# The pair swap of rotary embedding: a TensorE product replaced by four transfers issued from ScalarE

## The reference, cut to what matters

```python
def apply_partial_rope(x, cos, sin):           # layer a: the first 16 of 64 channels of a head
    half = ROPE_DIM // 2                       # 8
    x1, x2 = x[..., :half], x[..., half:ROPE_DIM]
    return concatenate([x1 * c - x2 * s, x2 * c + x1 * s, x[..., ROPE_DIM:]])

def rope(t, cos, sin):                         # layers 0 and 1: all 64 channels
    half = t.shape[-1] // 2                    # 32
    t1, t2 = t[..., :half], t[..., half:]
    return concatenate([t1 * cos - t2 * sin, t2 * cos + t1 * sin])
```

## Time and profile before

| | |
|---|---|
| device time, median of 3 (lowest to highest) | 2407.13 us (2404.87 to 2409.15) |
| the profiled execution's own time | 2409.83 us |
| its span, first to last instruction | 2407.0 us |
| mean granted TensorE clock | 0.978 |
| TensorE products busy | 2235.1 us (93%), 9994 instructions |
| VectorE busy | 1167.8 us (49%), 1815 instructions |
| ScalarE busy | 931.0 us (39%), 1577 instructions |
| GpSimd busy | 1138.5 us (47%), 1364 instructions |
| mean busy share of the 16 DMA engines, queue of SyncE / of ScalarE | 24.4% / 0.6% |

### The profile page before, as it was taken

How to read it: one execution, slowest core, us unless ns; L and a number is a source line. 1 busy time by engine, 2 the same in 40 slices (tenths; PEclk the granted TensorE clock), 3 DMA queues, 4 the chain that set the end, 5 groups by cost and what they waited for, 6 DMA issues and landing times.

```text
span 2407.0 us, 27365 instructions
## 1 busy us (share of the span) xinstructions
PE 2235.1 (93%) x9994; PEld 1697.5 (71%) x9994; DVE 1167.8 (49%) x1815; ACT 931.0 (39%) x1577; POOL 1138.5 (47%) x1364
## 2 busy tenths in 40 slices
PE   6899888998898999999999999889999999999996
PEld 4676556864465766888888788666668888887885
DVE  6786858237635434015319754363340153197542
ACT  3545633235533444233223731334442332237322
POOL 3563226541134422557547475443234575475751
PEclk8999999999999999999999999999999999999998
DMA  3222113220022212332232232212123322232321
GB/s 129 70 88 62 36 53 97 88 79 27 27 62 79 79 53 79 96 106 88 81 103 97 71 108 88 84 53 70 53 73 103 96 92 87 93 105 63 113 88 61
DMA packets 52981, 191.43 MB, mean 80 GB/s; under 512 B 6000, under 2 KB 6256, under 8 KB 52336
## 3 DMA queue, kind: packets, MB, share of 16 engines
q1 hardware_dynamic: 51552, 184.44, 24.4%
q10 hardware_dynamic: 1296, 5.24, 0.6%
HBM read 187.56 MB, written 2.10 MB: 79 GB/s over the span
## 4 chain that ended last, share of the span: by engine, by line
PE 77%; DVE 8%; ACT 6%; POOL 4%; issue 3%; DMA 2%; ACTq 0%; DVEq 0%; SPq 0%
PE proj L516 20%; PE proj L518 19%; PE proj L517 19%; POOL lower L468 4%; PE turned L512 3%; PE stat L512 2%; PE score L512 2%; PE score L516 2%; PE score L517 2%; PE score L518 2%; PE mix L512 2%; DMA raw_ring<-stream 2%; DVE small L1571 1%; PE ptp L727 1%; PE proj L512 1%
## 5 line engine op out<-in xcount | busy, mean ns | idle before, releaser
L468 POOL TENSOR_TENSOR lower<-raw_ring,upper 128x256 fp32r<-128x256 f32 x1360 | 1138.3, 870 | 1225.1 <-ACT upper L1062 1225.0
L516 PE MATMUL proj<-h,upper 128*128 128x512 f32 x1504 | 613.0, 408 | 30.4 <-issue 16.8
L518 PE MATMUL proj<-h,lower 128*128 128x512 f32 x1504 | 589.8, 392 | 0.0
L517 PE MATMUL proj<-h,upper 128*128 128x512 f32 x1504 | 589.0, 392 | 0.0
L1062 ACT ACTIVATE upper<-raw_ring 128x1024 fp32r<-128x1024 f32 x340 | 356.0, 1058 | 564.8 <-PE proj L516 373.3
L516 PEld LDWEIGHTS proj<-h,upper 128*128 128x128 f32 x1504 | 285.0, 189 | 96.6 <-issue 27.9
L518 PEld LDWEIGHTS proj<-h,lower 128*128 128x128 f32 x1504 | 284.1, 189 | 61.3
L517 PEld LDWEIGHTS proj<-h,upper 128*128 128x128 f32 x1504 | 285.2, 190 | 57.2 <-issue 4.3
L516 PE MATMUL proj<-y,upper 128*128 128x512 f32 x632 | 256.8, 406 | 10.8 <-ACT yf L1139 3.7
L518 PE MATMUL proj<-y,lower 128*128 128x512 f32 x632 | 252.0, 399 | 0.0
L517 PE MATMUL proj<-y,upper 128*128 128x512 f32 x632 | 251.6, 398 | 0.0
(11 more groups left out here) (368 smaller groups left out, 3246.7 us busy)
## 6 DMA issues: line engine op xcount, KB each, us to landing
raw_ring<-stream SPq DMA_DIRECT2D x340, 512.0 KB, 3.5
x<-x_in SPq DMA_DIRECT2D x4, 512.0 KB, 6.4
rows<-rows_in ACTq DMA_DIRECT2D x2, 1024.0 KB, 5.2
out<-x SPq DMA_DIRECT2D x8, 256.0 KB, 2.0
memraw<-mem_in SPq DMA_DIRECT2D x1, 1024.0 KB, 10.7
memraw<-mem_in ACTq DMA_DIRECT2D x1, 1024.0 KB, 4.8
rot<-tables_in ACTq DMA_DIRECT2D x2, 512.0 KB, 3.6
ws<-ws_in ACTq DMA_DIRECT2D x2, 256.0 KB, 5.6
```

What stands on the lines that cost most here:

```text
L468: ins = nc.gpsimd.tensor_tensor(lower[:, p % RING, a:b], raw_ring[:, p % RAWS, a:b], upper[:, p % RING, a:b].bitcast(FP32), ALU.subtract)
L516: first_ = nc.tensor.matmul(o, lhsT[0], rhs[0], start=start, stop=False)
L517: nc.tensor.matmul(o, lhsT[0], rhs[1], start=False, stop=False)
L518: return first_, nc.tensor.matmul(o, lhsT[1], rhs[0], start=False, stop=stop)
```

## The change

The permutation is no longer a product. `turn` and the wait for the bank `turned` are gone from TensorE's program. ScalarE gets a function `swap`, which issues four transfers from `nrm` to a second place in SBUF (`home`): `yf1` in layer a, `raw` in the layers 0 and 1, two buffers each. In layer a a transfer moves 8 partitions of 2 KB (16 KB); in the layers 0 and 1 it moves 32 partitions (64 KB). In layer a only 32 of the 128 rows are written, and one VectorE instruction clears both buffers beforehand. VectorE's `rotate` waits for the transfers instead of the product and reads `home` instead of the bank.

```diff
+        def swap(S, C, n, home, half):
+            m = C.next("turn")
+            act.wait_ge(*S.after("nrm", n))
+            if m >= 2:
+                act.wait_ge(*S.after("turned_used", m - 2))
+            src, dst = nrm[:, n % 2, :], home[:, m % 2, :]
+            for at in (0, half, HD, HD + half):
+                to = at + half if at % HD == 0 else at - half
+                act.dma_start(dst[to:to + half, :], src[at:at + half, :]).then_inc(swap_landed[m % 2], 16)
...
-        def heads(S, C, n, cols=SEQ, together=False):
-            for i in range(n + 1):
+        def heads(S, C, n, cols=SEQ, together=False, rotated=0):
+            n0 = C.n["head"]
+            for i in range(n + 2 if rotated else n + 1):
...
+                if 0 <= i - 2 < rotated:
+                    swap(S, C, n0 + i - 2, yf1, 8)
-                if i:
+                if 0 < i <= n:
                     root(S, C, 1.0 / HD, cols)
...
             def take_head():
                 k = C.next("head")
                 take(S, C, nrm[:, k % 2, :], keys_=[("nrm", k)], waits=[("nrm_used", k - 2)] if k >= head0 + 2 else [])
+                swap(S, C, k, raw, 32)
...
-        def rotate(S, C, n, dst, *keys_):
+        def rotate(S, C, n, dst, home, *keys_):
             m = C.next("turn")
             t = nrm[:, n % 2, :]
-            dve.wait_ge(*S.after("turned", m))
-            link(S, nc.vector.tensor_tensor(tmp[:, :], turned[:, :], rot[:, 1, :], ALU.mult), ("turned_used", m))
+            dve.wait_ge(swap_landed[m % 2], 64 * (m // 2 + 1))
+            link(S, nc.vector.tensor_tensor(tmp[:, :], home[:, m % 2, :], rot[:, 1, :], ALU.mult), ("turned_used", m))
...
+        link(S, nc.vector.memset(yf1[:, 0:2, :], 0.0))
...
-        def turn(S, C, swap, n):
-            m = C.next("turn")
-            pe.wait_ge(*S.after("nrm", n))
-            if m:
-                pe.wait_ge(*S.after("turned_used", m - 1))
-            mm(turned[:, :], swap, nrm[:, n % 2, :], True, True).then_inc(*S.mark("turned", ("turned", m)))
```

More of the change, by code:

```diff
@@ L302, in build @@
     stored = nc.alloc_semaphore("stored")
+    swap_landed = [nc.alloc_semaphore(f"swap_landed{r}") for r in range(2)]
     signals = Signals(nc, "run", plans)
@@ L644, in added_squares, with heads @@
             mm(stat[:, :], c("ones"), sq[:, t % 2, :], False, True).then_inc(*S.mark("summed", ("sq_used", t), ("sums", m)))
-        def turn(S, C, swap, n):
-            m = C.next("turn")
-            pe.wait_ge(*S.after("nrm", n))
-            if m:
-                pe.wait_ge(*S.after("turned_used", m - 1))
-            mm(turned[:, :], swap, nrm[:, n % 2, :], True, True).then_inc(*S.mark("turned", ("turned", m)))
-        def heads(S, C, W, jobs, rotate, cols=SEQ, together=None):
-            n0 = C.n["head"]
+        def heads(S, C, W, jobs, cols=SEQ, together=None):
             C.n["head"] += len(jobs)
-            def rotated(i):
-                if 0 <= i < rotate:
-                    turn(S, C, c("swap_a"), n0 + i)
             def summed():
@@ L670, in heads @@
                 jobs[4]()
-                rotated(0)
                 summed()
@@ L674, in heads @@
                 jobs[5]()
-                rotated(1)
-                rotated(2)
                 summed()
@@ L680, in heads @@
                     jobs[i]()
-                rotated(i - 3)
                 if i:
@@ L692, in attention @@
                 pe.wait_ge(*S.after("read", C.n["job"] - j))
-            if C.n["turn"]:
-                pe.wait_ge(*S.after("turned_used", C.n["turn"] - 1))
             def scores(kind, z, t, e, i):
@@ L778, in memory @@
             hkey = lambda k: ("h", f"mem{l}", k)
-            heads(S, C, W, [lambda i=i: full(S, C, W, f"mem{l}.k{i}", mh, hkey, MEM) for i in range(2)], 0, MEM)
+            heads(S, C, W, [lambda i=i: full(S, C, W, f"mem{l}.k{i}", mh, hkey, MEM) for i in range(2)], MEM)
             tokens(S, C, W, names(f"mem{l}.v", 2), mh, hkey, MEM, 2)
@@ L786, in pe_program @@
                 heads(S, C, W, [lambda n=n: full(S, C, W, n, h, hkey)
-                                for n in names("a.q", MT) + names("a.k", MT) + names("a.qm", 2)], 2 * MT,
+                                for n in names("a.q", MT) + names("a.k", MT) + names("a.qm", 2)],
                       together=lambda: group(S, C, W, names("a.q", 4), h, hkey))
@@ L803, in pe_program @@
                 hkey = lambda k: ("h", "b", k)
-                heads(S, C, W, [lambda n=n: full(S, C, W, n, h, hkey) for n in names("b.qm", 2)], 0)
+                heads(S, C, W, [lambda n=n: full(S, C, W, n, h, hkey) for n in names("b.qm", 2)])
                 for n in names("b.q", MT):
@@ L852, in pe_program @@
             full(S, C, W, "kr", h, None)
-            C.next("head")
-            turn(S, C, c("swap_b"), C.n["head"] - 1)
             for t in range(2):
@@ L874, in up @@
                     pass
[L876 to L882, removed]
+            for t in range(LH // 2):
+                up(QR * t, QR, 0)
             for t in range(2):
@@ L1238, in act_program @@
             if s == "a":
-                heads(S, C, 2 * MT + 2, together=True)
+                heads(S, C, 2 * MT + 2, together=True, rotated=2 * MT)
             else:
@@ L1531, in head_units @@
                 if 0 <= i - 2 < rotated:
-                    rotate(S, C, n0 + i - 2, dsts[i - 2], ready[i - 2])
+                    rotate(S, C, n0 + i - 2, dsts[i - 2], yf1, ready[i - 2])
                 if i < len(dsts):
@@ L1762, in dve_program @@
             dve.wait_ge(*S.after("nrm", n))
-            rotate(S, C, n, kr[:, :], ("tails_ready",))
+            rotate(S, C, n, kr[:, :], raw, ("tails_ready",))
             C.n["job"] += 2 * TB + LH
@@ L1767, in dve_program @@
                 n = C.next("head")
-                rotate(S, C, n, qr[:, t, :], ("tails_ready",))
+                rotate(S, C, n, qr[:, t, :], raw, ("tails_ready",))
             C.n["job"] += 2 * LH
```

## The result

The changed kernel takes 2426.24 us (median, 2425.13 to 2428.59). The kernel before, run beside it, takes 2406.68. The ratio is 1.0079 (95% interval 1.0065 to 1.0093): it is slower by 19.6 us, where 2406.0 was forecast and the range ended at 2416. The traced execution's span is 2426.8 us against 2407.0.

What follows compares the result with a forecast made beforehand. TensorE, with 77% of the chain, was taken as the bound where it is late; +6.9 us in layer a less 2 x (1.55 + 2.4) in layers 0 and 1 gave -1.0, forecast 2406.0 us, 8-in-10 range 2397 to 2416.

Steps and rivals of the forecast that it cites:

- What bounds layer a next: Layer a's heads: without the turn TensorE needs 6.35 us a tile, so the ScalarE-VectorE loop of 6.66 sets the period.
- The hold at the fifth copy: Start of layer a: the copy at 91.90 came after 7.54 us idle, awaiting a turned rotation; predicted to vanish.
- I take 1.00, from the only burst on the same queue: Layer a, ScalarE: four issues delay the logarithm by 1.00 us a tile, priced from a 1.78 us burst; ends 0 and 1.9.
- B: Time to issue one tile's four transfers on ScalarE in layer a: taken as 1.78 us, between 1.44 and 2.7.
- the up jobs: Layers 0 and 1, up jobs: the attention's release was to come at 22.6 instead of 25.0, 2.4 us earlier a layer.
- dear-issues rival: ScalarE between square and logarithm of layer a: costlier issues, 12 times the excess, 2421 us at 2.7 a burst; chance 0.17.
- The recorded sum: Whole kernel: total near zero at a burst of 1.9 us, passing +4.8 us near 2.3.
- Behind kr: Layers 0 and 1: TensorE no longer waits 0.69 for the kr copy and turns 0.86, saving 1.55 us a layer.
- Loads are seldom in these stretches: Up jobs of layers 0 and 1: the argument against swaps landing late, 5.5 us after issue instead of 2.0.
- late-landing rival: Up jobs: each swap lands 5.5 us after issue, not 2.0, losing 3.5 us a layer, 2412 us in total; chance 0.06.
- The clock: Layer a, TensorE: idling might drop its clock to 1.2 GHz, some 55 us longer if for all jobs; chance 0.04.
- The clearing of yf1: Ahead of layer a's loops, VectorE: clearing estimated between 0.3 and 1.1 us, of which 0.5 was counted.

## Why the prediction was wrong

**What bounds layer a next: right.** The loop of ScalarE and VectorE took over from TensorE, every copy was released by VectorE, TensorE idled at each sum of squares, and no landing was waited for. The hold at the fifth copy went too.

**"I take 1.00, from the only burst on the same queue": this step failed.** The burst of four took 2.61 us and not 1.78, so the delay was 1.84 and not 1.00. Its formula held: 0.14 + 2.61 + 0.06 is 2.81, measured 2.82, with 0.11 and 0.10 for its two small terms. With the right B the sum gives +16.9 for layer a; at the last sums it was +18.5 (167.02 against 148.49), the rest being the start (1.1, counted as 0.5) and two loops of 9.06 and 8.80. The rows used for the price were all transfers with one end in HBM. The run with the source in HBM shows that this made the difference (0.32 against 0.63), and the run with one large transfer that size did not. Of the 20 us between forecast and result, this term, times 12, is 10; the up jobs, below, are another 9. The loss against the kernel before lies in layer a alone, but the miss of the forecast does not.

**The bound was on record and the range did not reach it.** The dear-issues rival named the place and the price (12 times the excess), and at B = 2.7 gave 2421. It got 0.17 of the chance. That its bound of 2.7 came close to the measured 2.61 is luck: it was built on an issue that read HBM at the start of the program. The argument against it, that nothing on ScalarE had exceeded 0.46, spoke of other transfers. With no row of a transfer within SBUF, a term multiplied by 12 should have kept its upper end in the range. The recorded sum also flattered the middle: at B = 2.3 it is said to pass +4.8, but 12 x 1.52 - 5.1 - 7.9 is already +5.2 with the full gain of the layers 0 and 1, and that gain shrinks when issues are dear.

**Behind kr: right.** 1.87 us a layer were gained, 1.55 forecast. What was left out is the break in TensorE's rhythm around the turn: in the kernel before, the last product of kr and the second of the next job start 2.27 us apart (778.38 and 780.65), where two unbroken steps take 0.46, and that is 1.8 lost.

**The up jobs: wrong in size and sign.** -2.4 forecast, +2.3 and +2.0 measured. Two terms were too small: four issues of 64 KB took 2.44 and not 1.8, and the first swap landed in 4.46 (4.18 in layer 1) and not 2.0. "Loads are seldom in these stretches" was wrong where it mattered. The late-landing rival, for which the Trainium skill was named ("DMA: Bandwidth & Descriptors", "Rules for kernel authors": transfers from different engines interleave on the same 16 DMA engines), is borne out by the trace for the first swap of each layer, 4.46 beside a load against 2.1 alone, but not for the third and fourth, which met none. Holding the load back bought nothing, though. What pays is issuing faster, from two queues, and there the same section agrees too: it says that spreading saves only issue time, which was the cost here.

**The clock.** Mean clocks of 0.83 appeared, as feared, but in the loop they cost nothing, with 0.25 us to spare in every second loop. The cost was 1.6 us at the exit, which the sum had at nothing.

**The clearing of yf1.** Counted as 0.5, it cost 0.8. The copy of tile 2 came 1.1 us later than before; the other 0.3 lies within the scatter of the start.

## What to carry to other kernels

A transfer's issue is work of the engine that issues it. When it is put into an engine's program, its place in that engine's dependence loop decides: the same four issues cost 20 us between square and logarithm and about 1 us behind the exponential. Before trading a product for transfers, count issues and not bytes, and price them by a row with the same two ends. If none exists, leave the whole upper bound in the range. If several engines have idle queues, share the issues of one tile between them.

## What the runs showed of the hardware

- Issuing a transfer within SBUF took 0.63 us with 8 rows (1.25 for the very first one), 0.61 with 32 rows (0.51 for the first of four) and 0.49 with 128 rows, on ScalarE's queue; on SyncE's it took 0.62 and 0.59 with 8 and 32 rows. With 8 rows read from HBM it took 0.32, and a store from SBUF to HBM took 0.33. Why both ends in SBUF cost more stays open.
- In nine of the twelve loops of layer a ScalarE's sequencer started the first issue 0.10 to 0.11 us after the start of the activation ahead of it (0.05 twice, 0.41 once). One issue of 0.49 behind two activations added under 0.1 us to the loop, and four of 0.63 added 1.86.
- A swap of four times 64 KB landed 2.1 us after the start of its last issue when alone, and 3.9 to 4.5 when a 512 KB load was issued 0.1 to 1.2 us ahead of that issue.
- Two queues that issue at the same time slow each other little: 1.42 us for two against 1.15.
